# Two transformer blocks in fp32: half of the weight remainders of fourteen chunks on GpSimd

## What is computed

```python
# first block
h = rmsnorm(x, ffn_pre_norm[l])
u = causal_depthwise_conv(h @ w_up[l], conv_w[l], conv_b[l])      # "up": 1024 x 5632
gate, up = jnp.split(u, 2, axis=-1)
y = (jax.nn.gelu(gate, approximate=True) * up) @ w_down[l]
...
# second model, layer 0 and 1
gt, up = jnp.split(h @ w_gate_up, 2, axis=-1)                     # "gu0", "gu1"
y = (jax.nn.silu(gt) * up) @ w_down
...
m = jax.nn.silu(c) @ ada_w[layer] + ada_b[layer]                  # the conditioning, 1024 x 6144 each
```

## Time and profile before

| | us |
|---|---|
| median of 3 runs | 1054.32 (1052.58 to 1056.64) |
| profiled execution | 1054.75 |
| its span in the trace | 1053.0 |

### The profile page before, as it was taken

How to read it: one execution, slowest core, us unless ns; L and a number is a source line. 1 busy time by engine, 2 the same in 40 slices (tenths; PEclk the granted TensorE clock), 3 DMA queues, 4 the chain that set the end, 5 groups by cost and what they waited for, 6 DMA issues and landing times.

```text
span 1053.0 us, 19187 instructions
## 1 busy us (share of the span) xinstructions
PE 1027.0 (98%) x7842; PEld 975.0 (93%) x7842; DVE 804.9 (76%) x1380; ACT 594.6 (56%) x1029; POOL 161.6 (15%) x168
## 2 busy tenths in 40 slices
PE   7999999999999999999999999999999999999997
PEld 6987798999888997899999999998899999999997
DVE  5867789999997987588999688885668566674443
ACT  6686667666546675675444445543556466544443
POOL 0000033323201200024212001200110114111010
PEclk8999999999999999999999999999999999999999
DMA  9642336777695543157998788554444536774441
GB/s 369 248 143 98 103 131 227 301 273 284 256 391 228 165 152 125 74 207 278 375 370 340 283 326 306 170 193 160 126 155 142 218 122 226 278 278 150 166 166 40
DMA packets 33988, 227.49 MB, mean 216 GB/s; under 512 B 3779, under 2 KB 4076, under 8 KB 10220
## 3 DMA queue, kind: packets, MB, share of 16 engines
q1 hardware_dynamic: 33452, 223.63, 57.9%
q0 software_dynamic: 448, 2.63, 0.6%
HBM read 225.19 MB, written 2.63 MB: 216 GB/s over the span
## 4 chain that ended last, share of the span: by engine, by line
PE 80%; DVE 12%; ACT 5%; issue 1%; DMA 0%; POOL 0%; POOLq 0%; SPq 0%; ACTq 0%; DVEq 0%
PE psum L1474 20%; PE psum L1476 20%; PE psum L1475 20%; DVE w_lo L2219 5%; PE psum L1539 2%; PE psum L1542 2%; PE psum L1541 2%; PE psum L1883 2%; PE psum L1885 2%; PE psum L1884 2%; ACT w_hi L802 2%; DVE arena L2522 1%; DVE arena L2323 1%; DVE hid_lo L2304 1%; PE psum L2149 1%
## 5 line engine op out<-in xcount | busy, mean ns | idle before, releaser
L2219 DVE TENSOR_TENSOR w_lo<-raw,w_hi 128x1024 fp32r<-128x1024 f32 (+1 forms) x342 | 389.5, 1161 | 148.2 <-ACT w_hi L802 143.3
L802 ACT ACTIVATE w_hi<-raw 128x1024 fp32r<-128x1024 f32 (+1 forms) x342 | 335.4, 996 | 209.7 <-PE psum L1476 157.7
L1474 PE MATMUL psum<-h_hi,w_hi 128*128 128x256 f32 (+1 forms) x1144 | 325.5, 285 | 7.6 <-DVE w_lo L2219 3.0
L1475 PE MATMUL psum<-h_lo,w_hi 128*128 128x256 f32 (+1 forms) x1144 | 321.1, 281 | 0.0
L1476 PE MATMUL psum<-h_hi,w_lo 128*128 128x256 f32 (+1 forms) x1144 | 320.6, 280 | 0.0
L1474 PE MATMUL psum<-hid_hi,w_hi 128*128 128x256 f32 (+1 forms) x952 | 270.9, 285 | 0.6 <-DVE w_lo L2219 0.4
L1475 PE MATMUL psum<-hid_lo,w_hi 128*128 128x256 f32 (+1 forms) x952 | 268.1, 282 | 0.0
L1476 PE MATMUL psum<-hid_hi,w_lo 128*128 128x256 f32 (+1 forms) x952 | 268.1, 282 | 0.0
L1474 PEld LDWEIGHTS psum<-h_hi,w_hi 128*128 128x128 f32 x1144 | 215.3, 188 | 10.7 <-DVE w_lo L2219 5.4
L1475 PEld LDWEIGHTS psum<-h_lo,w_hi 128*128 128x128 f32 x1144 | 216.2, 189 | 0.7 <-issue 0.7
L1476 PEld LDWEIGHTS psum<-h_hi,w_lo 128*128 128x128 f32 x1144 | 215.9, 189 | 0.0
(11 more groups left out here) (294 smaller groups left out, 1215.7 us busy)
## 6 DMA issues: line engine op xcount, KB each, us to landing
arena<-in_ada SPq DMA_DIRECT2D x48, 1024.0 KB, 6.3
raw<-in_gu SPq DMA_DIRECT2D x44, 1024.0 KB, 6.9
raw<-in_ret_in SPq DMA_DIRECT2D x24, 1024.0 KB, 4.9
raw<-in_up SPq DMA_DIRECT2D x22, 1024.0 KB, 4.9
raw<-in_dn SPq DMA_DIRECT2D x32, 704.0 KB, 4.2
raw<-in_qkv SPq DMA_DIRECT2D x12, 1024.0 KB, 5.0
raw<-in_down SPq DMA_DIRECT2D x11, 1024.0 KB, 8.3
raw<-in_ret_o SPq DMA_DIRECT2D x8, 1024.0 KB, 4.8
```

Source lines behind the costliest of these rows:

```text
L802: nc.scalar.activation(w_hi[chunk % SPLIT_SLOTS][:, a:b], raw[chunk % RAW_SLOTS][:, a:b], ACT.Copy)\
L1474: nc.tensor.matmul(out, w[0], hc, start=start, stop=False, skip_group_check=True)
L1475: nc.tensor.matmul(out, w[0], lc, start=False, stop=False, skip_group_check=True)
L2219: tt(w_lo[s][:, a:b], raw[chunk % RAW_SLOTS][:, a:b], w_hi[s][:, a:b].bitcast(F32), ALU.subtract)\
```

## The change

The second halves of chunks 6 to 12 of `up` and of `gu0` are subtracted on GpSimd (`pool_lo`) and no longer on VectorE. GpSimd does it at the head of its step j, for chunk j + 3; it counts a new semaphore, `pool_split`, on which TensorE's `second_half` and SyncE's reload of the slot wait. VectorE counts `split_ready` by two for those chunks.

```diff
--- before.py
+++ after.py
@@ -104,6 +104,14 @@
 PH = lay_out_phases()
 ORDER = list(PH.values())
 CHUNKS = sum(ph.n for ph in ORDER)
+
+
+POOL_HALVES = {PH[name].chunk0 + c: 1 for name in ("up", "gu0") for c in range(6, 13)}
+
+
+def pool_halves_before(chunk):
+
+    return sum(c < chunk for c in POOL_HALVES)
 
 
 def phase_of(chunk):
@@ -351,7 +359,7 @@
         onehot_in, ident_in, band_out, bias_in, y_out = sem("onehot_in"), sem("ident_in"), sem("band_out"), sem("bias_in"), sem("y_out")
         raw_in = [sem(f"raw_in{i}") for i in range(RAW_SLOTS)]
         hi_ready, split_ready, half_done = sem("hi_ready"), sem("split_ready"), sem("half_done")
-        row_done = sem("row_done")
+        row_done, pool_split = sem("row_done"), sem("pool_split")
         lin_free = [sem(f"lin_free{i}") for i in range(2)]
         mla_units, v_rows, gate_turned = sem("mla_units"), sem("v_rows"), sem("gate_turned")
         rows_done, row_sq, row_copied, row_ms, row_root, row_diag, row_turned, row_x = (sem(n) for n in (
@@ -644,6 +652,8 @@
 
                     if chunk >= RAW_SLOTS:
                         sp.wait_ge(split_ready, step.n(lambda c: 2 * (ph.chunk0 + c - RAW_SLOTS + 1)))
+                    if chunk - RAW_SLOTS in POOL_HALVES:
+                        sp.wait_ge(pool_split, pool_halves_before(chunk - RAW_SLOTS) + 1)
                     src = dram[ph.name][bass.ds(step.n(lambda c: c * P), P), 0:n]
                     sp.dma_start(raw[slot][:, 0:n], src).then_inc(raw_in[slot], 16)
                 return load
@@ -694,6 +704,14 @@
         def _(pool):
             added = [0]
 
+            def pool_lo(chunk):
+                half, s = POOL_HALVES[chunk], chunk % SPLIT_SLOTS
+                of, c = phase_of(chunk)
+                a, b = of.halves(c)[half]
+                pool.wait_ge(hi_ready, 2 * chunk + half + 1)
+                nc.gpsimd.tensor_tensor(w_lo[s][:, a:b], raw[chunk % RAW_SLOTS][:, a:b], w_hi[s][:, a:b].bitcast(F32), ALU.subtract)\
+                    .then_inc(pool_split, 1)
+
             def add_squares(i):
 
                 sq, k0 = NORM[i][1], 0
@@ -713,6 +731,8 @@
                 at, cut = S * (j % 2), bass.ds(step.n(lambda c: c * S), S)
                 hid = ff["hid"][:, at:at + S]
 
+                if PH["up"].chunk0 + j + 3 in POOL_HALVES:
+                    pool_lo(PH["up"].chunk0 + j + 3)
                 pool.wait_ge(gelu_ready, step.n(lambda c: c + 1))
                 nc.gpsimd.tensor_tensor(hid, ff["u"][:, 2 * at + S:2 * at + 2 * S], ff["g"][:, at:at + S], ALU.mult)\
                     .then_inc(hid_ready, 1)
@@ -722,6 +742,8 @@
             def remainder(base):
                 def one(step):
                     j = step.j
+                    if base == FT and PH["gu0"].chunk0 + j + 3 in POOL_HALVES:
+                        pool_lo(PH["gu0"].chunk0 + j + 3)
                     pool.wait_ge(hid_hh, step.n(lambda c: base + c + 1))
                     cut = bass.ds(step.n(lambda c: c * S), S)
                     nc.gpsimd.tensor_tensor(hid_lo[:, cut], ff["hid"][:, S * (j % 2):S * (j % 2) + S], hid_hi[:, cut].bitcast(F32),
@@ -1476,12 +1498,18 @@
                 return nc.tensor.matmul(out, w[1], hc, start=False, stop=stop, skip_group_check=True)
 
             def weights(chunk, step, ph):
-                pe.wait_ge(split_ready, step.n(lambda c: 2 * (ph.chunk0 + c) + 1))
+                if POOL_HALVES.get(chunk) == 0:
+                    pe.wait_ge(pool_split, pool_halves_before(chunk) + 1)
+                else:
+                    pe.wait_ge(split_ready, step.n(lambda c: 2 * (ph.chunk0 + c) + 1))
                 s = chunk % SPLIT_SLOTS
                 return w_hi[s], w_lo[s]
 
             def second_half(ph, step):
-                pe.wait_ge(split_ready, step.n(lambda c: 2 * (ph.chunk0 + c) + 2))
+                if POOL_HALVES.get(ph.chunk0 + step.j) == 1:
+                    pe.wait_ge(pool_split, pool_halves_before(ph.chunk0 + step.j) + 1)
+                else:
+                    pe.wait_ge(split_ready, step.n(lambda c: 2 * (ph.chunk0 + c) + 2))
 
             def by_feature(ph, step, first_tiles=None, rhs=None, k0=lambda c: 0, midway=None, free=True):
 
@@ -2213,11 +2241,11 @@
                 at = (lambda f: f(chunk)) if step is None else (lambda f: step.n(lambda c: f(ph.chunk0 + c + 1)))
                 s = chunk % SPLIT_SLOTS
                 for half, (a, b) in enumerate(of.halves(c)):
-                    if ahead in (0, 1) and half != ahead:
+                    if ahead in (0, 1) and half != ahead or POOL_HALVES.get(chunk) == half:
                         continue
                     dve.wait_ge(hi_ready, at(lambda k: 2 * k + half + 1))
                     tt(w_lo[s][:, a:b], raw[chunk % RAW_SLOTS][:, a:b], w_hi[s][:, a:b].bitcast(F32), ALU.subtract)\
-                        .then_inc(split_ready, 1)
+                        .then_inc(split_ready, 2 if chunk in POOL_HALVES else 1)
 
             def rstd(i):
```

## The result

The changed kernel takes 1063.22 us (median of 4 runs, 1062.32 to 1063.43) against 1054.24 (1052.58 to 1056.64) for the kernel before, a ratio of 1.008 with a 95% interval of 1.0062 to 1.0098: by the ratio 8.4 us slower, between 6.5 and 10.3 (the two medians lie 9.0 apart). The forecast was 1063.6, range 1056 to 1071. The profiled execution took 1062.32 us with a span of 1060.5, 7.5 us above the span before.

A forecast was written before the change was run, and what follows sets the result against it. gu0 was taken as bound by TensorE (5.66 us a chunk) and VectorE (5.63) at once; 4.8 us for gu0 plus 4.5 for up, 9.3 on 1054.75, gave 1064.05, and 1063.6 for the median; range 1056 to 1071.

The forecast's parts named there:

- gu0, chunk 6 / chunk 7 later by: TensorE starts chunk 6 of gu0 at 496.7 instead of 494.72, and chunk 7 1.5 us later.
- up, chunk 9: In up, an added TensorE wait of 0.9 us at chunk 9.
- up, chunk 11 / 13: In up, TensorE waits 1.0 us more at chunk 11, and 1.7 at chunk 13 with the loop late.
- up, ScalarE's loop without / with reductions: In up, ScalarE's loop through GpSimd's product grows from 4.40 us to 5.6, or 6.2 to 6.8 with reductions.
- The exclusion: VectorE instructions with both sources in SBUF and GpSimd instructions exclude each other; the new subtract holds VectorE 2.2 us.
- VectorE's first half of `w_lo`: In gu0, the VectorE subtract expected to wait 2.2 us while GpSimd's new subtract holds the resource.
- the line through the earlier trace: GpSimd's 128x1024 subtract takes 2.4 us, from 0.74 for 128x256 plus 0.55 per 256 more columns.
- longer ones of 1 us are not priced: TensorE's clock stays at 1.00 through 1.2 us stalls, so stalls longer by 1 us got no clock cost.
- Rival 1: Exclusion costs nothing for a long instruction; VectorE's relief shortens stops in gu0 and up by 1.8 us: 1052.5; chance 0.12.
- Rival 2: Only gu0 pays, 4.8 us; up's slack swallows the loop: 1059.1; chance 0.14.
- Rival 3: The subtract is 3.0 us long, four times a 128x256, adding 7.7 us: 1071.3; chance 0.14 with worse.
- Rival 4: Waits on GpSimd make TensorE's second half late in up, 0.5 us for seven chunks; inside the range, no separate chance.

The follow-up runs named there:

- the write-only kernel: The change in up alone, with each GpSimd subtract replaced by a 128x2560 memset and those halves not computed; 1056.87 us against 1056.24, ratio 1.0011.
- up alone: Only the seven chunks of up moved to GpSimd, gu0 as in the kernel before; 1058.45 us, ratio 1.0045 to the kernel before.
- the doubled kernel: The change in gu0 alone, with GpSimd's 128x1024 subtract done twice, once into unused space; 1075.11 us against 1053.94 before, ratio 1.0202.
- the product first: The change in up alone, with GpSimd's product ahead of its subtract in each step; 1057.9 us against 1053.94 before, ratio 1.004.
- the kernel with both reorderings: Kernel before, gu0's conditioning pieces in steps 6 to 21, plus ScalarE and VectorE reordered in steps 4 to 6 of up; 1055.3 us, ratio 1.001.
- half width: The change in gu0 alone, GpSimd taking only the last 512 columns of each half and VectorE the first 512; 1056.95 us against 1056.24 before.
- gu0 alone: Only the seven chunks of gu0 moved to GpSimd, up as in the kernel before; 1059.88 us against 1053.71, ratio 1.0055.
- the kernel with the later pieces: Kernel before, nothing moved to GpSimd, gu0's 16 conditioning pieces in steps 6 to 21 instead of 4 to 19; 1053.71 us, ratio 1.0.

## Why the prediction was right, step by step

| step | forecast | measured |
|---|---|---|
| GpSimd subtract, 1024 columns | 2.4 us | 2.38 in gu0, mean 2.48 |
| of it held on VectorE | 2.2 | 2.30 - 0.16 = 2.14 |
| VectorE's step in gu0 | 6.3 | 6.28 |
| gu0, chunk 6 / chunk 7 later by | 2.0 / 1.5 | 1.67 / 1.20 |
| gu0, chunks 8 to 12 | 0.65 each | 6.31 - 5.66 = 0.65 |
| gu0 in all | 4.8 | 4.6; 4.7 alone |
| up, chunk 7 | 0.9 | 0.78 |
| up, chunk 9 | 0.9 | none; clock, about 1.3 |
| up, chunk 11 / 13 | 1.0 / 1.7 | 0.5 / 1.4 |
| up, ScalarE's loop without / with reductions | 5.6 / 6.2 to 6.8 | 5.64 to 5.79 / 6.66 |
| up in all | 4.5 | 3.0; 3.9 alone |
| profiled execution | 1064.05 | 1062.32 |

**The exclusion** is the step on which everything rested, and it held: it was read off a reduction that was 0.54 us too long and scaled by four, and the runs give 2.14 for 2.2. It is not quite the instruction's whole length: 2.14 of 2.38 us, as 0.54 of 0.74 before. Only the victim was another: I had named VectorE's first half of `w_lo`, and except in chunk 6 it is the two-column add in front of it. The claims add up to the same, as the text said they would. The duration came from the line through the earlier trace rows; it is 0.02 off. The estimate of 2.25 us worked out from the Trainium skill (GPSIMD Engine Reference, "Performance versus the Vector engine") is 0.13 below what was measured.

**gu0** is right in mechanism and within 0.2 us in size. The start was put 0.3 us too high. VectorE's first half of chunk 6 starts at 495.86 and takes 3.42 us, so it is held for 2.2 as forecast; but it starts 495.86 - 486.51 = 9.35 us behind the mark where before it was 493.45 - 483.57 = 9.88, so 0.5 of the delay was there before under another name, and 1.67 is left.

**up** is right in its mechanism, wrong in one term, and near in its sum partly by luck. The loop on ScalarE has the two lengths forecast, and the longer one comes from the first reduction holding the product, as the text said. The stops of chunks 11 and 13 are there, both smaller (term mis-sized: 1.0 measured 0.5, 1.7 measured 1.4; why is not shown). The step that failed is "longer ones of 1 us are not priced": the stop before chunk 7 grew from 1.19 to 1.96 us idle, and the clock behind it fell. In 184 to 188 us 23 matmuls ran where the write-only kernel ran 34 of about 0.12 us each, so 11 x 0.12 = 1.3 us. That took the place of the stop of chunk 9, as TensorE came there late by itself. So one missed term and one that fell away cancel, and that is luck. Of the two measured sums, 3.9 is the one to hold against 4.5: up to the stop of chunk 13 the changed kernel and the one with up alone run alike (both start it at 221.29), and the 0.9 us between them arise behind it (last section).

**The rivals.** Rival 1 (nothing excludes) falls by the held add and the doubled kernel; its size of the relief, 1.2 to 1.4 us in gu0, was if anything low (2.0). Rival 2 (only gu0 pays) falls by up alone, 1.0028 at the least. Rival 3 (3.0 us) falls by 2.38. Rival 4 (TensorE's second half late in up) shows in no stop of the changed kernel; it came only with the product first (0.86 us idle, released by GpSimd).

## What to carry to other kernels

Before moving work from VectorE to GpSimd, count the time in which one holds the other and not each engine's own busy time: a moved 128x1024 subtract saved VectorE 1.14 us and held it for 2.14 in gu0. Count both directions: in up the moved work held VectorE hardly at all, but made GpSimd's own next instruction late and let VectorE hold that. Look for the price in a pair that already overlaps in the trace (one instruction longer than its twins by a fixed amount), and multiply. Work that GpSimd only writes, or that VectorE reads from PSUM, did not pay that price here. And where a stop of TensorE is lengthened, allow for the clock behind it as a term of its own.

## What the runs showed of the hardware

**The clock after a stop.** It fell behind 1.96 us of idle (183.49, changed kernel), 2.41 (182.75, the kernel with both reorderings) and 2.45 (501.92, half width), behind 1.99 with up alone and behind 1.92 (220.44, product first). It stayed at 1.00 behind 1.65 (183.90, write only), but also behind 2.58 (499.33, changed kernel) and 2.59 (496.65, gu0 alone):

```profile
500.00:504.00 4.00, 4.00 (x36) 4.00 (x35) 3.96 (x5) 2.23 (x4) 1.96 (x1) 1.00 0.66 277
```

With the doubled subtract it fell behind a stop of the same 2.58 us at the same place (495.61; 0.59 and 23 matmuls from 496 to 500 us). So the length of the stop alone doesn't decide, and what does is open. Where it fell and TensorE was the engine that the others waited for, it cost about 1.3 us; with the doubled subtract it fell several times more without changing the step of 8.40 us, which VectorE sets.

**TensorE's pace.** With no stop, and the clock granted at 1.00 throughout, the same 58 us of gu0 hold 495 matmuls before and with up alone, but 486 in the write-only kernel for up:

```profile
510.00:568.00 58.00, 58.00 (x486) 58.00 (x485) 57.62 (x84) 27.42 (x42) 12.17 (x11) 1.00 0.98 375
```

The starts lie 120.0 ns apart in that stretch against 117.8 before, 2%, or 0.1 us a chunk of 48 matmuls. The change from one spacing to the other comes at other places in other runs: from 241 to 261 us the changed kernel ran 172 matmuls, and before and with up alone it was 169. Over a phase of 22 chunks this moves a span by up to 2 us, about the scatter between runs of one kernel. The 0.9 us between the two measures of up (3.0 and 3.9) come from it, and so do the 1.6 us by which the unchanged gu0 of the write-only kernel for up is longer than the others. It also explains the two paces of the prediction: 48 x 120.0 ns are 5.76 us, 48 x 117.8 are 5.66, so they are no property of up and gu0. In the kernel with the later pieces up itself ran at the shorter one (470 matmuls in 190 to 245 us, 461 before). The cause is not known.
